# Rebuilding the order of the third mixer in a two-layer plus hybrid-layer block on one core

## The reference

```
h = rms_norm(x); proj = h @ w_in          # 1440 columns: 512 xr, 512 yg, 256 c_q, 128 c_kv, 32 k_rope
xf, xb = causal and anti-causal 4-tap convolution of xr
hf, hb = rg_lru(xf), rg_lru(xb, reversed) # gates sigmoid(x @ w), a = exp(rate * r), b = sqrt(1 - a*a) * i * x, scan
lru_out = (hf + hb) * gelu(yg)
q = rms_norm(c_q) @ w_uq                  # 8 heads of 64 + 32
k = [rms_norm(c_kv) @ w_uk, k_rope], v = rms_norm(c_kv) @ w_uv
q, k = rms_norm over the 96 columns of each head, times a gain; the last 32 rotated by position
mla_out = softmax(q k^T / sqrt(96)) v
x = x + [rms_norm(lru_out), rms_norm(mla_out)] @ w_out
x = x + memory attention: q from rms_norm(x) @ w_mem_q, k, v from rms_norm(mem) @ w_mem_kv, 4 heads of 128
x = x + feed-forward with a 3-tap convolution
```

## Time and profile before

| | us |
|---|---|
| median of three runs (1611.47 to 1612.77) | 1612.36 |
| the profiled execution | 1612.5 |
| its span, first to last instruction | 1610.7 |
| TensorE busy | 1480.4 (92%) |
| VectorE busy | 1186.1 (74%) |
| ScalarE busy | 691.0 (43%) |
| GpSimd busy | 169.4 (11%) |

### The profile page before, as it was taken

The page is one execution under the profiler, slowest core; times in us unless marked ns, Lnnn a source line. Parts: engine busy times, 40 slices in busy tenths (PEclk is TensorE's granted clock), DMA queues, the critical chain, the costliest instruction groups (busy, mean ns, idle before and its releaser), DMA issues.

```text
span 1610.7 us, 26753 instructions
## 1 busy us (share of the span) xinstructions
PE 1480.4 (92%) x10982; PEld 1373.5 (85%) x10982; DVE 1186.1 (74%) x1881; ACT 691.0 (43%) x1098; POOL 169.4 (11%) x100
## 2 busy tenths in 40 slices
PE   1999999989999999999899899999985698799998
PEld 1999989789999899999886799998843496699998
DVE  6888977858778798786686665655728656589998
ACT  2443444544433444334544443344444444444443
POOL 0000000000000000010000000000724233023433
PEclk8999998999999999999999999999987799889999
DMA  9977773264786656755421446543310124235452
GB/s 391 416 308 295 298 284 131 84 277 175 302 314 266 237 225 246 313 210 224 167 92 53 157 157 235 191 173 126 136 47 20 66 78 158 79 118 185 175 192 79
DMA packets 32328, 309.28 MB, mean 192 GB/s; under 512 B 3496, under 2 KB 5800, under 8 KB 7504
## 3 DMA queue, kind: packets, MB, share of 16 engines
q1 hardware_dynamic: 32208, 307.59, 49.6%
HBM read 306.51 MB, written 1.06 MB: 191 GB/s over the span
## 4 chain that ended last, share of the span: by engine, by line
PE 83%; DVE 10%; ACT 2%; issue 2%; DMA 1%; POOL 0%; SPq 0%; DVEq 0%; ACTq 0%; POOLq 0%
PE bank L744 13%; PE bank L616 12%; PE bank L612 12%; PE bank L613 12%; PE bank L664 6%; PE bank L662 6%; PE bank L667 6%; PE bank L629 2%; PE bank L582 2%; PE bank L809 1%; PE bank L787 1%; DVE tmp L1529 1%; DVE WL L1511 1%; PE bank L774 1%; DMA PR<-in_stream 1%
## 5 line engine op out<-in xcount | busy, mean ns | idle before, releaser
L1511 DVE TENSOR_TENSOR WL<-ring,WH 128x1024 fp32r<-128x1024 f32 x380 | 465.6, 1247 | 65.4 <-ACT WH L1026 63.0
L1026 ACT ACTIVATE WH<-ring 128x1024 fp32r<-128x1024 f32 x420 | 429.6, 1053 | 154.4 <-PE bank L744 61.5
L612 PE MATMUL bank<-XH,WH 128*128 128x256 f32 x1680 | 409.7, 283 | 1.4 <-ACT WH L1026 1.4
L613 PE MATMUL bank<-XL,WH 128*128 128x256 f32 x1680 | 406.6, 281 | 0.0
L612 PEld LDWEIGHTS bank<-XH,WH 128*128 128x128 f32 x1680 | 316.5, 188 | 7.6 <-issue 6.0
L613 PEld LDWEIGHTS bank<-XL,WH 128*128 128x128 f32 x1680 | 317.1, 189 | 1.0 <-issue 1.0
L616 PE MATMUL bank<-XH,WL 128*128 128x256 f32 x1680 | 233.6, 282 | 2.9 <-DVE WL L1511 2.9
L616 PEld LDWEIGHTS bank<-XH,WL 128*128 128x128 f32 x1680 | 213.7, 189 | 3.3 <-DVE WL L1511 3.3
L662 PE MATMUL bank<-GH,WH 128*128 128x256 f32 x840 | 203.9, 281 | 1.7 <-DVE GL L1635 1.7
L664 PE MATMUL bank<-GL,WH 128*128 128x256 f32 x840 | 203.9, 282 | 0.0
L1110 ACT ACTIVATE SG<-bank 128x256 f32<-128x256 f32 x88 | 33.8, 384 | 385.3 <-PE bank L616 361.8
(11 more groups left out here) (264 smaller groups left out, 1892.4 us busy)
## 6 DMA issues: line engine op xcount, KB each, us to landing
ring<-in_stream SPq DMA_DIRECT2D x132, 1536.0 KB, 6.4
scr<-in_stream SPq DMA_DIRECT2D x15, 1536.0 KB, 10.8
PR<-in_stream SPq DMA_DIRECT2D x15, 1536.0 KB, 8.1
att<-in_stream SPq DMA_DIRECT2D x15, 1536.0 KB, 9.9
ring<-in_stream SPq DMA_DIRECT2D x9, 1024.0 KB, 4.9
ring<-in_stream SPq DMA_DIRECT2D x11, 512.0 KB, 3.5
kf_mix<-in_stream SPq DMA_DIRECT2D x2, 1536.0 KB, 16.5
con<-in_consts SPq DMA_DIRECT2D x1, 2112.0 KB, 16.2
```

Source lines behind the costliest of these rows:

```text
L612: pe.matmul(o, part(WH, u, k), XH[:, k, :], start=(k == 0), stop=False)
L613: pe.matmul(o, part(WH, u, k), XL[:, k, :], start=False, stop=False)
L1026: act.activation(part_all(WH, u), raw(u), ACT.Copy).then_inc(*mark("high", u))
L1511: dve.tensor_tensor(part_all(WL, u), raw(u), part_all(WH, u).bitcast(F32), ALU.subtract)\
```

## The change

It reorders the stretch from the third input projection to the memory queries, on all engines.

1. Latent queries and keys are made inside `win2`: a pair of query heads behind each of units 6 to 9, key pairs and values ahead of unit 10. The query product takes the latent without its norm; the factor of that norm cancels in the norm of the head, and only the epsilon is corrected (`q_eps`). `mla` weights are loaded ahead of the third item of `win2`.
2. The query norm is no longer multiplied in: `q_stats` makes its sums per token as 20 products of one column, and the root goes into the scale of the exponentials (`q_rate`) and of the maximum (`q_neg`).
3. The rotation of a query uses a second product with swapped weight columns instead of a swap matmul. The rope part of the key, the same in all heads, is rotated once (`key_rope`) and copied into each head by an identity product of 32 rows.
4. GpSimd's convolution goes to VectorE (`lru_convs`, both directions side by side), ScalarE making the first tap; the rotation's multiplies are gone from GpSimd.
5. The memory: `mem` is loaded during the feed-forward before, its squares are made there, its norm sum ahead of `win2`. `wmk` and three of four units of `wmv` are made in and around the latent attention (`lead`, `fill`), the last `wmv` unit behind `wout2`. The sum of the norm ahead of `wmq` is made between the units of `wout2`. `wout2` has two banks instead of four.
6. The exponentials of the decay, the variance and its square root move into the heads of the attention; the scans from heads 1 to 4 to heads 4 and 5.
7. VectorE makes all low halves but those of the last `w2` (18 units move from GpSimd).

```diff
-        return "pool" if name[1] == 4 else "dve"
-    if name[0] in ("w1", "w3", "win0", "wout0", "win1", "wout1"):
-        return "dve"
-    return "pool" if name[1] % 2 else "dve"
+    return "pool" if name[0] == "w2" and name[1] == 4 else "dve"
...
+            def q_pair(p):
+                take(4 + p % 2, "q_turned", p)
+                take(6 + p % 2, "q_turned", p)
+                if p == 0:
+                    pe.wait_ge(*landed(("mla", 0)))
+                    pe.wait_ge(*at("act_copied", "win2", 1))
+                for i in range(2):
+                    cols = slice(i * S, (i + 1) * S)
+                    for k in range(2):
+                        pe.matmul(bank[4 + p % 2][0:96, cols], uq[:, k, 2 * p + i, :], PR[:, 8 + k, body], start=(k == 0), stop=(k == 1))
+                    for k in range(2):
+                        last = pe.matmul(bank[6 + p % 2][64:96, cols], uq_swapped[:, k, 2 * p + i, :], PR[:, 8 + k, body],
+                                         start=(k == 0), stop=(k == 1))
+                last.then_inc(*mark("q_product", p))
...
+            def k_pair(p):
+                take(4 + p % 2, "k_copied", p)
...
+                for i in range(2):
+                    cols = slice(i * S, (i + 1) * S)
+                    pe.matmul(bank[4 + p % 2][0:64, cols], uk[:, 2 * p + i, :], lat[:, 2, :], start=True, stop=True)
+                    last = pe.matmul(bank[4 + p % 2][64:96, cols], ident[64:96, 64:96], kr, start=True, stop=True)
...
+            def win2_and_attention():
...
+                take(7, "stat_root", "mem")
+                norm_sum("mem")
+                passes = projection("win2", *norm_parts("attn2"))
+                proj_first("win2", passes)
+                for j in range(2, 5):
+                    unit("win2", passes, j)
+                norm("ckv")
+                rope_of_key()
+                unit("win2", passes, 5)
+                for p in range(4):
+                    unit("win2", passes, 6 + p)
+                    q_pair(p)
+                for p in range(4):
+                    k_pair(p)
+                values()
+                unit("win2", passes, 10)
+                q_stats()
+                k_sums()
+                unit("win2", passes, 11)
+                k_spread()
+                lru_products(0)
+                lru_products(1)
+                memory = projection("wmk", *norm_parts("mem"))
+
+                def lead():
+                    unit("wmk", memory, 0)
+                    unit("wmk", memory, 1)
+
+                def fill(h, k):
+                    if (h, k) in ((0, 2), (1, 1)):
+                        unit("wmk", memory, 2 + h)
+                    if (h, k) in ((2, 1), (4, 1)):
+                        memory_value(h // 2 - 1)
+
+                attention("m", lambda h: [("rotated", h // 2), ("head_normed", "mk", h // 2), ("v_copied", 1)], fill=fill, lead=lead)
+                memory_value(2)
+                take(4, "stat_root", "lru")
+                norm_sum("lru")
+                head_sum("memk")
...
             gates(1)
-            head_squares("mk", [("k_copied_act", 6), ("k_copied_dve", 7)])
-            head_root("mk")
-
+            split_to(first_unit("wmk") + 1)
             act.wait_ge(*at("lru_gate", 1, 1, 3))
             act.wait_ge(*at("lru_rate"))
             for d in range(2):
...
+                    rated(ACT.Tanh, d, c, LRU[d]["A"][:, c, :], "lru_tanh")
             act.activation(gel, gel, ACT.Gelu_apprx_tanh).then_inc(*mark("gelu"))
...
+            split_to(first_unit("wmk") + 3)
             load_table(ACT.Exp)
 
-            def early(h):
-                if h == 6:
+            def with_head(h):
+                if h == 0:
+                    act.wait_ge(*at("rotated", 3))
+                    for j in range(2):
+                        memory_key(j)
+                    act.wait_ge(*at("lru_tanh", 1, 3))
+                    for d in range(2):
+                        for c in range(4):
+                            rated(ACT.Exp, d, c, LRU[d]["R"][:, c, :], "lru_decay")
+                if h in (1, 2):
+                    memory_key(1 + h)
+                if h < 5:
+                    split_to(first_unit("wmv") + (0, 1, 2, 3, 3)[h])
+                if h == 3:
+                    head_squares("memk", [("act_copied", "wmk", 3)])
+                    for d in range(2):
+                        act.wait_ge(*at("lru_var", d))
+                        act.activation(LRU[d]["A"], LRU[d]["A"], ACT.Sqrt, scale=-1.0).then_inc(*mark("lru_mult", d))
+                    load_table(ACT.Exp)
+                if h in (5, 6):
+                    split_to(first_unit("wout2") + h - 4)
+                if h == 7:
                     load_table(ACT.Sqrt)
-                    squares("lru", lambda c: [("lru_out", c)])
-
-            attention("m", early)
+                    for c in range(4):
+                        square("lru", c, lambda c: [("lru_out", c)])
...
+            def q_rope(p):
+                dve.wait_ge(*at("q_squared", p))
...
+                ins.then_inc(*mark("q_turned", p))
+                dve.wait_ge(*at("q_turned", p))
...
+            for j in range(12):
+                split_to(min(u0 + j + PARTS, u0 + 11))
+                if j in (1, 2):
+                    norm_scale("mem", range(4 * j - 4, 4 * j))
+                if j == 4:
+                    key_rope()
+                if j == 5:
+                    norm("ckv")
                 if 5 <= j < 9:
...
+                    lru_convs(j - 5)
+                if 7 <= j < 11:
+                    q_rope(j - 7)
...
+            def with_head(h):
+                if 1 <= h < 3:
+                    variance(h - 1)
+                if h < 5:
+                    split_to(first_unit("wmv") + (0, 1, 2, 3, 3)[h])
+                if h in (4, 5):
+                    states(h - 4)
+                if h in (5, 6):
+                    split_to(first_unit("wout2") + h - 4)
```

515 lines of the change are left out of this document (272 added, 243 removed).

## The result

The changed kernel takes 1600.01 us (median of 4 runs, 1599.44 to 1601.51), the kernel before 1612.24 (1611.47 to 1612.77) on the same chip: ratio 0.992, 95% interval 0.9907 to 0.9932. It is 12.2 us faster. That lies inside the range of 1571 to 1603 that the prediction gave with its rivals, but outside the 1578 to 1594 of its own sum, and it is less than half of the 26.7 us of that sum. The profiled execution took 1600.39 us, with a span of 1598.4.

The account below looks back on a forecast made before the run. The changed stretch was taken as bound by a chain of small steps without dense work beside it. Terms -21.2 + 17.2 - 27.7 + 5 = -26.7 gave 1585.8 us; own range 1578 to 1594, with rivals 1571 to 1603.

Parts of the forecast that it names:

- transposes after 1235 us: Sign of being wrong: first transposes of the latent attention later than this; they were forecast near 1222 to 1226.
- The other signs: TensorE idle some 6 us before transposes, heads 6 us on the mean, first 10, GpSimd at 22 low halves, among others.
- Start of the projection, +1.7: Third input projection: VectorE makes unit 1's low half later, so the two first products end at 1130.1 instead of 1128.4.
- Projection and latents: From 1130.1 to 1207 on TensorE, then ScalarE's chain; first transposes at 1222 against 1243.2, so -21.2 us.
- Clock, +5: Half clock behind small products: one fall of 3 us in the new stretch and 2 more in the heads.
- Attention, +17.2: Latent attention heads grow from 34.6 to 51.8 us with memory units and added ScalarE and VectorE work.
- After the attention, -27.7: From the attention's last product to the end of the memory query projection: 55.6 us instead of 83.3.
- (a): Latent attention heads become the bound, added blocks not overlapping: 64.1 instead of 51.8 us, so 1598; 0.24 together with (d).
- (b): Better than summed: no fall of the clock and no collision with GpSimd, -8 us, 1577; chance 0.12.
- (c): Clock stays at its lower level from the key pairs to the first transposes and in heads: +47, 1633; chance 0.05.
- (d): VectorE bounds the projection, its operations half as long again through its last 26 us: 1597; 0.24 together with (a).
- The drain that the Trainium skill adds to each table load: ScalarE: 1.38 us behind each load; three loads in the open chain would make the sum 1590; not added.

Follow-up runs that it names:

- e4_same: The changed kernel run once more, unaltered, on another chip: 1596.54 us in one run.
- e2_low: The changed kernel, but GpSimd again makes the low half of unit 1 of win2: 1594.05 us.
- e6_nostats: The changed kernel with all but one of the twenty one-column products left out, and the query norms with them: 1587.46 us.
- e8_spread: The changed kernel with wmq starting in banks 2 and 3, GpSimd making unit 1's low half, and the one-column products spread in groups: 1585.79 us.
- e1_bank: The changed kernel, but the wmq products start in banks 2 and 3 instead of 0 and 1: 1595.99 us.
- e13_layout: The changed kernel with tiles behind the constants moved to within 32 bytes of where the kernel before has them: 1592.75 us.
- e15_spread: e8_spread with the tile placement of e13_layout: 1586.96 us.
- e11_all: e8_spread with GpSimd's two input products in the heads also moved to VectorE, directly ahead of the scans: 1589.73 us.
- e3_dense: The changed kernel with 36 extra full products, results unread, put between the one-column products, key sums and spreads: 1611.51 us.
- e14_before: The kernel before with eight unused constant columns, so its tiles lie exactly where e13_layout has them: 1613.99 us.

## Why the forecast was too low

The direction held, and so did the main idea: dense work now covers the chain. The sum was 14.4 us too low in the spans. The prediction named transposes after 1235 us as a sign of being wrong, and they came at 1237.8 (1234.3 in e4_same). The other signs held: 51.5 us for the heads, the first of 9.3, TensorE idle for 6.9 us ahead of them, 22 low halves on GpSimd. By its own steps:

- **Start of the projection, +1.7.** The place was right: from the root to the low half of unit 1 are 11.2 us, 11.1 were forecast. But the wait is 2.88 us, because TensorE reached it 8.3 us behind the root and not 9.4. e2_low measures 3.1 for the whole of it, 1.4 more than entered. The clock fell behind the wait as well (3.4 us); that is counted with the clock.
- **Projection and latents.** The stall at the third query pair was forecast as 1.4 and is 1.40. Query products take 0.50, not 0.45 (pairs in 4.0 us), 1.6 more in all. The Trainium skill ("TensorEngine Tiling (Array Packing)", Key Properties) says that changing the tiling mode drains the engine. By it the prediction weighed the key rows' 0.60 for these pairs; the trace lies between the two. One-column products took 4.4, not 5.0; key pairs 9.55 for 9.6, with a wait of 0.52 in them. Without the clock the stretch from root to transposes is 105.8 (106.8 if the half clock in the last wait is left out), and the forecast had 105.9 (1222 less 1116.1): errors of both signs cancel in it. The chain on ScalarE from the scores on is 14.6 us for 14.9, but without the table load of 1.3 that was in the sum.
- **Clock, +5: this step failed.** I allowed 3 us for the latents. The stretch holds 22.6 us at half clock, of which 20.5 with TensorE at work: 10.2 to 11.3 us of cost, 7.3 to 8.3 too little (4 to 5 in e4_same, which had one fall fewer). The rows that I took it from the earlier trace rows showed a fall behind small products, and I priced a stretch with more of them by the one fall seen, once. e6_nostats shows what I missed: the one-column products, which I had entered at 5.0 us only, bring most of the fall of 10.2 us at the key sums with them. e8_spread shows that it is these products where they stand, in a row of small ones, and not by themselves.
- **Attention, +17.2.** 51.4 us for 51.8 and 2 of clock, so 2.4 less. GpSimd beside the scans cost 2.15 in the first four and some 0.9 in the second, near the 3.2 entered. That the total came out so near is partly luck: the mean clock of 0.80 is some 20 us at half clock, and I had priced one short fall.
- **After the attention, -27.7: 6.5 too much.** 62.1 instead of 55.6. The schedule left out a bank: `wmq` 0 needs the one that holds the memory values. e1_bank gives 3.5 to 4.0 of it back. The schedule's own rows add up to 41.6 at the end of `wmv` 3 where it says 41.8, which changes nothing. 1.27 us is a wait for VectorE's add at the second product of `wout2`; the rest I have not traced.
- **What I never entered: 4.6 us ahead of the change.** I costed all other stages at nothing because their instructions stay. Their operands moved. 2.5 us of it are the second mixer, in every run, and e13_layout gives 1.9 of them back; 2.3 are the first mixer, which scatters by more than that from run to run. In all the placement is worth 3.8 to 7.3 us in the changed kernel, by which of its two batches e13_layout is held against, and nothing clear in e15_spread.
- Behind `wmq` the changed kernel has 2.5 us less than before (247.1 us to the end, for 249.6), for which I had nothing. The half clock there is 3.4 us shorter, which would be 1.7 of it.

In the spans: 4.6 ahead of the change, 8.1 from the root to the transposes (7.3 to 8.3 of clock, the rest of everything else), -2.4 in the attention, 6.5 behind it, -2.5 behind `wmq`: 14.3 of the 14.4 us that lie between the forecast gain of 26.7 and the spans' 12.3. The two negative terms are luck: without them the time would have left the range.

Of the rivals, (a), that the heads are the bound at 64 us, is out: they took 51.5. (b), without a fall and without the collision, is out, both came. (c), half clock throughout, is out in size but was the right kind: the clock is the largest single error. (d), VectorE as the bound of the projection, is out: the stall is 1.40. The drain that the Trainium skill adds to each table load ("ScalarE: Activation LUTs", What ACT_TABLE_LOAD costs) did not show here either: the load at 1228.99 starts as the tanh ends, and its gelu follows 1.30 later. One of the three loads did not come: the tanh (L1487) starts directly behind the halves.

```profile
1223.78 2.00 ACT L1125 ACTIVATE WH<-ring 128x1024 fp32r<-128x1024 f32 x2
1225.67 1.70 ACT L1487 ACTIVATE scr<-scr,rates 128x256 f32<-128x256 f32 x4
...
1228.99 1.28 ACT L1497 ACT_TABLE_LOAD   x1
1230.29 1.06 ACT L1497 ACTIVATE PR<-PR 128x1024 f32<-128x1024 f32 x1
```

Still open: why the second mixer takes 142.4 us in one program and 144.9 in the other, what share of the fall the key products and sums around the one-column products have, why e11_all has two kinds of runs, and whether one-column products spread singly would end the fall (e8_spread halves it).

## What to carry over

When a chain of small steps is moved beside dense work, the sum of durations can be right to a microsecond and the time still be wrong: price the clock from every stretch of small products that the new order makes, and count a very small product by what follows it. Write the banks into the hand schedule beside the engines, since a bank held by a copy at the end of a queue is a wait that no duration shows. A change of a parameter or constant tile moves every tile behind it; to compare two versions of a stage, keep the placement the same.

## What the runs showed of the hardware

- The granted clock falls to a half with TensorE busy without a gap, behind 40 records of one column, or within them (e2_low: from 1191.2 us, the records from 1188.17 to 1193.9) (e6_nostats with two of them: no fall there, 3.4 us of one 8 us later). 36 dense products between the sparse ones did not hold it (e3_dense), and 16 such records between a unit and a query pair brought no fall (e8_spread, 1159.82). A stretch at half clock costs about half its length: 105.8, 105.7, 105.8 us are left of three stretches of 117.0, 113.9 and 113.8.
- The same stream of products takes 276, 279 or 280 ns for each by where its operands lie in SBUF (e13_layout and e14_before, the changed kernel, the kernel before, all at full clock), and the segments of the first two mixers repeat to 0.3 us or less between two different programs with the same placement (123.4, 198.6, 215.9, 143.0, 198.0 us in e13_layout; 123.1, 198.4, 215.9, 143.0, 197.9 in e14_before).
- VectorE's scans take 2.44 us for four alone and 4.59 beside a GpSimd product of 1024 columns.
- The tanh behind the sigmoids came without a table load (row 1225.67).
